# The shift of the routed rows added by TensorE, with shorter comparisons, in a hand-ordered two-layer trunk

## The reference, cut to what matters

```python
h = rms_norm(x, g) * (1 + scale) + shift          # scale and shift from the conditioning, one pair for context, one for latent
scores = sigmoid(h @ w_router)                    # 384 x 16
sel = (scores + b_router).reshape(-1, 4, 4)
best = argmax(sum(top_k(sel, 2)[0], -1), -1)      # the best of 4 groups by its two best scores
idx = best * 4 + top_k(sel[best], 2)[1]           # two experts of that group
w = scores[idx] / sum(scores[idx])
gate = sum(one_hot(idx, 16) * w[..., None], 1)
a = silu(h @ w_gate[e]) * (h @ w_up[e]) * gate[:, e]
y = sum over e of a @ w_down[e]
```

## Time and profile before

| | before |
|---|---|
| median of 3 runs | 1133.17 us (1132.31 to 1133.34) |
| the profiled execution | 1131.33 us |
| its span, first to last instruction | 1129.5 us |
| its mean granted TensorE clock | 0.978 |
| exponential of the route stage, layer 0 and layer 1 | 258.58 us and 793.74 us |
| first product of expert 0, layer 0 and layer 1 | 287.51 us and 818.45 us |

### The profile page before, as it was taken

How to read it: one execution, slowest core, us unless ns; L and a number is a source line. 1 busy time by engine, 2 the same in 40 slices (tenths; PEclk the granted TensorE clock), 3 DMA queues, 4 the chain that set the end, 5 groups by cost and what they waited for, 6 DMA issues and landing times.

```text
span 1129.5 us, 16096 instructions
## 1 busy us (share of the span) xinstructions
PE 1062.4 (94%) x5963; PEld 844.3 (75%) x5965; DVE 850.6 (75%) x1177; ACT 693.4 (61%) x885; POOL 181.8 (16%) x202
## 2 busy tenths in 40 slices
PE   7999998896999999999999999899699999999997
PEld 4798454683788888888868985568388888888876
DVE  5345656767999888888865546865899988888896
ACT  2323555652687777777724256755367777777764
POOL 0335200343111111110040011000301111111002
PEclk8999999997999999999999999999799999999998
DMA  9997888256999999999599463004799999999951
GB/s 353 345 345 220 321 300 282 71 171 258 354 370 365 368 376 375 373 374 386 212 389 280 149 188 128 1 1 152 299 362 375 367 370 384 375 375 369 367 195 58
DMA packets 83201, 321.99 MB, mean 285 GB/s; under 512 B 22560, under 2 KB 27054, under 8 KB 70332
## 3 DMA queue, kind: packets, MB, share of 16 engines
q1 hardware_dynamic: 67232, 285.58, 68.6%
q0 software_dynamic: 14800, 32.30, 8.5%
q10 hardware_dynamic: 1100, 3.23, 0.7%
HBM read 310.15 MB, written 30.59 MB: 302 GB/s over the span
## 4 chain that ended last, share of the span: by engine, by line
PE 84%; DVE 7%; ACT 4%; DMA 2%; issue 2%; SPq 1%; POOL 0%; DVEq 0%; ACTq 0%; POOLq 0%
PE bank L1266 16%; PE bank L1258 16%; PE bank L1259 16%; PE bank L1133 3%; PE bank L960 3%; PE bank L956 3%; PE bank L930 3%; PE bank L953 3%; PE bank L1319 2%; PE bank L1147 2%; DMA ring<-in_w_in 2%; PE bank L1025 2%; PE bank L1165 2%; PE bank L990 1%; PE bank L1066 1%
## 5 line engine op out<-in xcount | busy, mean ns | idle before, releaser
L1744 ACT ACTIVATE work_r<-ring 128x4096 fp32r<-128x4096 f32 x93 | 338.1, 3635 | 121.4 <-PE bank L1259 109.9
L2340 DVE TENSOR_TENSOR ring_r<-ring,work_r 128x4096 fp32r<-128x4096 f32 x92 | 404.2, 4417 | 2.8 <-ACT work_r L1744 2.8
L1258 PE MATMUL bank<-work_r 128*128 128x512 f32 x768 | 305.2, 397 | 4.7 <-issue 3.2
L1259 PE MATMUL bank<-work_r 128*128 128x512 f32 x768 | 300.1, 391 | 0.0
L1266 PE MATMUL bank<-ring_r,work_r 128*128 128x512 f32 x768 | 193.8, 394 | 0.0
L1258 PEld LDWEIGHTS bank<-work_r 128*128 128x128 f32 x768 | 144.8, 188 | 35.2 <-issue 4.0
L1266 PEld LDWEIGHTS bank<-ring_r,work_r 128*128 128x128 f32 x768 | 143.7, 188 | 32.4
L1259 PEld LDWEIGHTS bank<-work_r 128*128 128x128 f32 x768 | 144.4, 188 | 28.8
L2626 POOL DMA_INDIRECT work<-hscr,idx x32 | 39.9, 1247 | 280.9 <-PE bank L1319 253.5
L1587 ACT ACTIVATE work_r<-ring 128x512 fp32r<-128x512 f32 (+1 forms) x48 | 28.8, 603 | 71.4 <-PE bank L960 71.3
L2024 DVE TENSOR_TENSOR ring_r<-ring,work_r 128x512 fp32r<-128x512 f32 (+1 forms) x48 | 32.1, 676 | 50.7 <-ACT work_r L1587 50.6
(11 more groups left out here) (282 smaller groups left out, 1582.9 us busy)
## 6 DMA issues: line engine op xcount, KB each, us to landing
ring<-in_w_gate SPq DMA_DIRECT2D x32, 2048.0 KB, 10.1
ring<-in_w_up SPq DMA_DIRECT2D x32, 2048.0 KB, 10.2
ring<-in_w_down SPq DMA_DIRECT2D x32, 2048.0 KB, 10.4
ring<-in_w_ada SPq DMA_DIRECT2D x24, 2048.0 KB, 9.6
ring<-in_w_in SPq DMA_DIRECT2D x4, 2048.0 KB, 16.6
yscr<-hT POOLq DMA_DIRECT2D x2, 3072.0 KB, 12.8
ring<-yscr SPq DMA_DIRECT2D x6, 1024.0 KB, 7.2
ring<-in_w_out SPq DMA_DIRECT2D x4, 1280.0 KB, 6.5
```

The lines of the kernel that those rows point to most:

```text
L1258: mm(b[:], x_hi[:, k, :], hi[:, k, half, :], start=(k == 0), stop=False)
L1259: last = mm(b[:], x_lo[:, k, :], hi[:, k, half, :], start=False, stop=False)
L1744: A_(w_hi[:, slot % 2, :], ring[slot][:], ACT.Copy).then_inc(s_hi, 1)
L2340: tt(ring_r[slot][:], ring[slot][:], w_hi[:, slot % 2, :].bitcast(F32), ALU.subtract).then_inc(s_lo, 1)
```

## The change

The sums, the transposes and their order. TensorE now adds the shift: it turns the rows of one half of the columns for all three token tiles and leaves the banks open, then adds in each bank the product of one row: `inv_rows` (the reciprocal of `ns`, one value per token) times the row of the shift. ScalarE's copy multiplies by `ns`, so the shift itself comes out. `inv` is made by VectorE, turned by three small matmuls and copied by ScalarE. GpSimd's three additions and their semaphores are gone. ScalarE issues the store of each half row tile right behind its copy.

The shift's part of the logits: GpSimd folds `swr` by three halving additions, so that one matmul takes the place of eight.

The comparisons: who beats whom is taken as a difference of one masked comparison and its transpose, which saves one operation on 192 and one on 48 elements, and joins the two that followed.

The exponential stands before all row copies on ScalarE. The halves of expert 0's high part become quarters (two before `op6`, one before `op7`, one behind the stores); of the low part one quarter stands at `op6` and three in one operation behind `tokens_rest(0)`. The one-hots of part 3 go behind that operation, and `by_slot(3)` moves from the gate products to the `up` products. In layer 0 the fillers stand in another order. In layer 1, SP holds its third load (`w_up` of expert 1) until the first gather has landed, as layer 0 did before; until now layer 1 held only the load behind it.

```diff
-    return ["A010"], ["A011"], ["B010", "B011"], ["A18", "A19", "B18", "B19"]
+    return ["A010"], ["A011", "B010", "A18"], ["B011"], ["B18", "A19", "B19"]
...
-        n += ["router", "shiftw", "routerT"] + [f"hr{t}{h}" for t in range(NT) for h in range(2)]
+        n += ["router", "routerT"] + [f"hr{t}{h}" for h in range(2) for t in range(NT)]
...
-                            if p == 0 and isinstance(i, int) and (e, kind) == (1, 2 if l else 1):
+                            if p == 0 and isinstance(i, int) and (e, kind) == (1, 1):
                                 sp.wait_ge(gathers(l, 0)[0][0], gathers(l, 0)[1][0] + 16)
...
+                pe.wait_ge(s_swr, 6 * (l + 1))
+                mm(bW, ones, swr[:, 0, :], start=True, stop=True)
                 sums_of_added(l)
...
-                b = fill_begin((l, "shiftw"))
-                for k in range(KT):
-                    last = mm(b[:, 0:NT * NE], ones, swr[:, k, :], start=(k == 0), stop=(k == KT - 1))
...
-                    turn4((l, f"hr{t}{h}"), lambda k: hT[:, 4 * h + k, t * P:(t + 1) * P])
+                def rows_turned_half(h):
+                    pe.wait_ge(s_zgain, KT * l + 4 * h + 4)
+                    for t in range(NT):
+                        b = fill_begin((l, f"hr{t}{h}"))
+                        for k in range(4):
+                            mm(b[:, k * P:(k + 1) * P], hT[:, 4 * h + k, t * P:(t + 1) * P], ident, is_transpose=True,
+                               start=(k == 0), stop=False, skip_group_check=True)
+                def shift_added(h):
+                    for t in range(NT):
+                        r = slice(32 * t, 32 * t + 1)
+                        last = mm(bank((l, f"hr{t}{h}"))[:], inv_rows[r, :], shift_rows[1 if t == 0 else 0][r, 512 * h:512 * h + 512],
+                                  start=False, stop=True, skip_group_check=True)
+                        filled((l, f"hr{t}{h}"), last)
+                rows_turned_half(0)
+                pe.wait_ge(s_inv, 3 * l + 1)
+                for t in range(NT):
+                    last = mm(bI[32 * t:32 * t + 32, 0:P], inv[:, t:t + 1].to_broadcast([P, 32]), ident, start=True, stop=True,
+                              skip_group_check=True)
+                last.then_inc(s_inv, 1)
+                rows_turned_half(1)
+                pe.wait_ge(s_shin, 32 * (l + 1))
+                pe.wait_ge(s_inv, 3 * l + 3)
+                shift_added(0)
+                shift_added(1)
...
+                act.wait_ge(s_inv, 3 * l + 2)
+                A_(inv_rows[0:96, :], bI[0:96, 0:P], ACT.Copy).then_inc(s_inv, 1)
+                act.wait_ge(s_rexp, 2 * l + 1)
+                A_(rw[:, 0, :], rw[:, 0, :], ACT.Exp, scale=-1.0).then_inc(s_rexp, 1)
...
-                row_copies(0)
-                act.wait_ge(s_logit, l + 1)
-                A_(rw[:, 0, :], rw[:, 0, :], ACT.Exp, scale=-1.0).then_inc(s_rexp, 1)
-                row_copies(1)
-                row_copies(2)
-                row_store(0)
-                for j in route[0]:
-                    ada_row(l, j)
-                first_expert_high(l, 1).then_inc(s_hi, 1)
-                row_store(1)
-                row_store(2)
-                for j in route[1] + route[2] + route[3]:
+                for h in range(2):
+                    for t in range(NT):
+                        half = slice(512 * h, 512 * h + 512)
+                        copy((l, f"hr{t}{h}"), hrow[t][:, half], 512, scale=ns[:, 1, t:t + 1])
+                        read_out(act, (l, f"hr{t}{h}"))
+                        act.dma_start(hscr[t * P:(t + 1) * P, half], hrow[t][:, half]).then_inc(s_hscr, 16)
+                first_expert_high(l, 3)
+                act.wait_ge(s_feh, 4 * (l + 1))
+                act.sem_inc(s_hi, 1)
+                for j in (j for step in route for j in step):
                     ada_row(l, j)
...
-                    chain(tt(c1, spread4(x, "i"), spread4(x, "j"), ALU.is_equal))
+                    chain(tt(c1, spread4(x, "i"), spread4(x, "j"), ALU.is_ge))
                     chain(tt(c1, c1, before.unsqueeze(1).to_broadcast([P, n, EPG, EPG]), ALU.mult))
-                    chain(tt(c2, spread4(x, "i"), spread4(x, "j"), ALU.is_gt))
-                    chain(tt(c1, c1, c2, ALU.add))
-                    chain(nc.vector.tensor_reduce(g4(dst), c1, AX.X, ALU.add))
+                    chain(tt(c2, c1, c1.rearrange("p g j i -> p g i j"), ALU.subtract))
+                    chain(nc.vector.tensor_reduce(g4(dst), c2, AX.X, ALU.add))
+                    place_no = cv("iota")[:, 0:EPG].unsqueeze(1).to_broadcast([P, n, EPG])
+                    chain(stt(g4(dst), g4(dst), EPG - most, place_no, ALU.add, ALU.is_lt))
...
-                    for q in range(2, NPS if p else NPS - 1):
+                    for q in range(2, NPS if p else NPS - 2):
                         onehots(q)
...
-                    if p == 0:
-                        first_expert_low(0)
                     tokens_rest(0)
                     if p == 0:
-                        first_expert_low(1).then_inc(s_lo, 1)
+                        first_expert_low(1, 4).then_inc(s_lo, 1)
+                        onehots(NPS - 2)
                         onehots(NPS - 1)
...
+                for i, k in enumerate((KT // 2, KT // 4, KT // 8)):
+                    g.wait_ge(s_swr, 6 * l + NT + i)
+                    nc.gpsimd.tensor_tensor(swr[:, 0:k, :], swr[:, 0:k, :], swr[:, k:2 * k, :], ALU.add).then_inc(s_swr, 1)
...
-                for t in range(NT):
-                    read_out(g, (l, f"hr{t}0"))
-                    read_out(g, (l, f"hr{t}1"))
-                    nc.gpsimd.tensor_tensor(hrow[t], hrow[t], shift_rows[1 if t == 0 else 0], ALU.add).then_inc(s_hrow, 1)
```

More of the change, by code:

```diff
@@ L1302, in experts @@
                     by_slot(0)
+                    if p == 0:
+                        for j in route[3][0:1]:
+                            ada(j)
                     by_slot(1)
                     if p == 0:
-                        for j in route[3]:
+                        for j in route[3][1:]:
                             ada(j)
@@ L2160, in out_low, with first_expert_low @@
                     tt(w_low[:, x, c], w[:, x, c], out_hi[half].bitcast(F32), ALU.subtract).then_inc(s_outw_lo, 1)
-                def first_expert_low(half):
-                    v.wait_ge(s_hi, chunk_no(l, 0, 0, 0) + 1)
-                    x = slice(CW // 2 * half, CW // 2 * half + CW // 2)
+                def first_expert_low(first, end):
+                    v.wait_ge(s_feh, 4 * l + end)
+                    x = slice(CW // 4 * first, CW // 4 * end)
                     return tt(ring_r[0][:, x], ring[0][:, x], w_hi[:, 0, x].bitcast(F32), ALU.subtract)
@@ L2379, in experts @@
                     onehots(1)
+                    if p == 0:
+                        for j in route[1] + route[2]:
+                            ada(l, j)
                     slots(1)
                     if p == 0:
-                        for j in route[2]:
+                        for j in route[3][0:1]:
                             ada(l, j)
```

58 lines of the change are left out of this document (26 added, 32 removed).

## The result

| | before | changed |
|---|---|---|
| median | 1133.26 us (4 runs) | 1141.59 us (1140.37 to 1141.85, 4 runs) |
| profiled execution, its span | 1131.33, 1129.5 us | 1140.37, 1138.2 us |
| mean granted TensorE clock | 0.978 | 0.972 |

The ratio is 1.0075, 95% interval 1.0061 to 1.0089: slower, where 1129.7 was forecast, and outside the range. A second set of runs gave 1.0069 (1.0049 to 1.0088).

The account below looks back on a forecast made before the run. TensorE, busy 94%, was taken as the bound, with only its idle or slowed time in the two route stages winnable. Layer 0's 2.7 plus layer 1's 1.0 less 0.25 gave 3.45: median 1129.7 us, range 1125.8 to 1134.0.

Parts of the forecast that it names:

- T: Start of tokens_rest in each route stage; layer 0 forecast 280.3 to 281.4 instead of 286.77, layer 1 278.8 instead of 282.56.
- Before the mask: VectorE's route work: three long operations shrink by 5.65 without GpSimd's additions, and the mask ends at 262.5 instead of 269.8.
- Rival 4: VectorE's three long operations are long of themselves: mask at 268.2, costing 0.4 in layer 1, nothing in layer 0; no chance given.
- The shift on TensorE: Six one-row matmuls behind the transposes, 0.86 each, 5.2 us; they end at 263.9, A010 and A011 at 267.7.
- ScalarE: Six turns of copy, store issue and waits, 1.15 us each (1.0 to 1.5); A010's row copy ends at 268.2.
- From the rank to T, layer 0: B010, A18, rank at 271.0, gather 272.7, then A19, B19 and tokens: T at 280.3 to 281.4.
- Layer 1: Its route stage: T at 278.8 instead of 282.56, or 276.9 at full clock; half of the gather's 8 us store wait taken.
- What is given back: Behind T: VectorE's weights at T + 14.75, TensorE waits 3.2 us for them, 2.7 us lost per layer.
- GpSimd's halving: GpSimd's three small new additions may hold up VectorE in the op steps: 0.25 us for both layers.
- rival 3: Six stores on ScalarE's queue delay the fillers' row copies: slower from a turn of 1.45 us, up to 1137; chance 0.13.
- Rival 1: TensorE's clock stays full behind the rank: layer 0 gains 3.7, layer 1 2.9, median 1126.8; chance 0.22.
- Rival 2: Half stores end late, ScalarE's turn is 1.35, or the clock falls at A010: almost nothing won, 1132 to 1134; chance 0.20.

Follow-up runs that it names:

- c0: The changed kernel unaltered, run and profiled a second time: 1139.39 us, 1.0069 of the kernel before.
- x3: Changed kernel with ScalarE's copy of the first filler's row (A010, A110) moved from behind all six stores to behind the fourth: 1133.69 us, 1.0018.
- z5: Changed kernel with 18 unread matmuls filling TensorE's wait for the row copy, ahead of B010 and B110: 1142.03 us, 1.0078.
- y5: Changed kernel with 12 unread matmuls filling TensorE's wait for the weights of the slots: 1138.82 us, 1.006.
- x4: Changed kernel with GpSimd's three halving additions moved behind its masked bias of the next layer: 1139.12 us, 1.0066.
- y1: Changed kernel with both x1's move of the weights and x3's move of the row copy: 1123.44 us, 0.9927.
- x1: Changed kernel with VectorE's eight operations for the weights of the slots moved ahead of its wait for the rank: 1128.23 us, 0.9968.
- z2: y1 with three stores of whole rows (512 KB) in place of six of half rows: 1122.73 us, 0.9907.
- z4: z1 with SP in layer 0 also holding expert 1's gate weight until the first gather has landed: 1122.36 us, 0.9903.
- x2: Changed kernel with the one-hots of part 3 put back ahead of tokens_rest: 1131.19 us, 0.9993.
- y3: Changed kernel keeping shift, logits, comparisons, half-row stores and high-part quarters; filler order, part-3 one-hots, by_slot(3), SP's hold undone, low part partly: 1127.64 us, 0.9961.
- z1: y1 with layer 1's row copy of A111 also moved, to behind the fifth store: 1121.57 us, 0.9905.

## Why the prediction was wrong

Between the forecast (3.45 gained) and the first profile (8.73 lost) lie 12.2 us: 3.1 in T of layer 0, 0.8 in T of layer 1, 4.3 behind the weights, and the rest in two stretches that no term covered. For c0 the same parts are 4.8, 0.6, 3.2 and 2.1.

- **Before the mask: right.** L2264 and its neighbours fell to 0.2 to 0.5 us; the mask ends at 264.90 - 2.2 = 262.7, forecast 262.5. Rival 4 falls. The Trainium skill, "SBUF — State Buffer", SBUF: two separate sides, says that a VectorE operation with two SBUF inputs and a GpSimd operation that reads SBUF share one pair of ports, which the one that starts first holds for its whole instruction; this trace agrees (1.78 to 0.21 on 48 elements once GpSimd's additions are gone).
- **The shift on TensorE: mis-sized, on the good side.** I took 0.86 for each of six matmuls, 5.2; they take 2.0 together, since those of different row tiles run side by side. The Trainium skill, "TensorE: Matmul & The Clock Gate", Part 3: Packing small matmuls — row/col tiling, says that matmuls in different row groups overlap, which the prediction did not use. This trace agrees: three start within 0.01 us at 261.00.
- **ScalarE: right.** Turns 1.09 to 1.14 apart (forecast 1.15), A010's row copy ends at 270.70 - 2.2 = 268.5 (forecast 268.2).
- **From the rank to T, layer 0: the step that failed first.** I had TensorE busy until 267.7 and waiting half a microsecond; with the shift's real size it is done at 264.5 and idle for 4.04, until the row copy that comes when I had reckoned. So the overlap failed: work that I had laid over the row copy was not there. I had put half clock only behind the rank, and one job of it; in fact B010 and A18 ran at it already (4.6 together for 2.6), so the rank came 2.2 later than 271.0. From the rank to the gather I had 1.7 and it takes 3.0, and B011, which stands ahead of `by_slot(1)`, keeps TensorE waiting 2.39 for VectorE. T gained 2.3 to 0.6 instead of 5.4. x3 shows that the row copy's place is the cause; z5 shows that the clock at B010 and A18 alone is not, since the rank then comes at the forecast's time and T does not.
- **Layer 1: nearly right.** T gained 2.9 and 3.1 for 3.7. TensorE was done early here too, waited 4.18 for the row copy, and ran B110 and B111 at half clock (1.11 and 1.12). What the prediction calls layer 1's fillers of 4.05 (L1311) are ten matmuls that nobody reads. The gather did not wait for the stores: they land in 2.2 us there, 8.3 before. I had taken half of the 8.
- **What is given back: right in size, wrong in its end.** Weights 14.6 behind T (14.75 forecast), last product of `up` +2.7 in each layer. But the sum stopped at the wait's length. Behind it the clock fell, which cost another 1.6 to 2.7 in each layer, 4.3 in all in the profile after and 3.2 in c0; the trace of y5 takes just that away. It is a term that the sum lacked altogether.
- **GpSimd's halving: 0.25 forecast, nothing found** (x4).
- **What no term of mine covers:** layer 0's route starts 0.9 to 2.2 late, and the end of its experts costs 1.4 to 2.1. The first lies between -1.4 and +2.6 in the other kernels, with nearly the same work ahead of it. At the second, TensorE waits 2.4 to 3.4 us for nothing that the profile shows, before the change too (2.38). Behind it the clock falls in some executions and not in others; windows and waits say so (the changed kernel, then y1), but what decides it stays open. The expectations of x1 and c0 call it a wait of TensorE for its own code; no run shows that.

```profile
576.93 0.76 PE L1282 MATMUL bank<-work_r 128*128 128x512 f32 x1 [3.15 <-issue]
```

```profile
575.00:580.00 5.00, 3.07 (x7) 2.48 (x8) 3.10 (x2) 0.00 (x0) 0.21 (x1) 0.63 1.05 384
```

```profile
564.10 0.47 PE L1282 MATMUL bank<-work_r 128*128 128x512 f32 x1 [2.46 <-issue]
```

```profile
565.00:570.00 5.00, 5.00 (x25) 3.94 (x23) 2.85 (x3) 0.14 (x1) 0.57 (x1) 1.00 1.05 383
```

- **The rivals.** Slower came out, and the condition that rival 3 named was met in layer 0 (T gained 2.29 and 2.67 were given back), but not in layer 1 (2.91 and 2.70). Over both layers it makes 0.2 us and not 8.7, and its mechanism did not come, as the turn was not 1.45 or more. The stores on ScalarE's queue did delay the row copy, by what I had reckoned; what I had not reckoned is that TensorE would idle for it, and what an idle TensorE then does to its clock. Rival 1, full clock, was refuted by the windows. Rival 2's early fall of the clock, at A010, did come in some traces: A010 and A011 took 5.33 in z2 and 5.34 in z4 (there behind a wait of 1.65) and 3.64 in the other eleven of the changed kernels; in layer 1 the two jobs took 5.34 in c0, x2, x3, x4 and z2. In c0 it cost nothing there, since TensorE then waited 2.20 for the row copy instead of 4.18, and T gained 3.1. In c0, y3 and z2 the first twelve transposes of layer 0 took 2.7 to 2.8 us at half clock, and the second twelve 1.5 to 1.7: the clock came back in between. The Trainium skill, "TensorE: Matmul & The Clock Gate", Part 4: PE-mode transpose, says that the full clock does not engage for transposes, which do not count as busy in the same way. These rows do not agree: c0's granted clock was 0.50 from 257 to 259 and 1.00 from 260 to 261, with transposes and three small matmuls of 0.42 us on TensorE. Rival 2's six small stores did not land later than three large ones (7.5 us in y1, 8.7 in z2).

## What to carry to other kernels

When a change lets an engine wait less at one place, look at every list behind it that is worked off in order, and put each item where its user waits for it: here one row copy and eight small operations, moved, turned 0.75% slower into 0.7% faster (y1), 0.95% with one copy more (z1). Price a new wait of TensorE not by its length alone but also by the slow work behind it. And a term that was taken too large can hide a wait: check a sum again with its uncertain terms at their lower bound.

## What the runs showed of the hardware

- An idle stretch of 2.5 us of TensorE was followed by half clock, with 1.6 to 2.7 us of lost time; filled with matmuls that nobody reads, by none (y5). One of 0.74 us was followed by it as well (x2, layer 0, 1.5 us lost), one of 0.75 was not (x2, layer 1), and stretches of 2.4 to 2.5 us at the end of a loop were in some executions only.
- In c0 the granted clock came back from 0.50 to 1.00 while TensorE ran transposes, and in ten of thirteen profiles of changed kernels layer 0's 24 transposes ran at the full rate (1.47 and 1.53 us for twelve).
- Six matmuls of one row by 512 fp32 columns, in three row groups, took 2.0 us together; three at a time start within 0.01 us.
- Beside a load of 2 MB a store of 256 KB landed 7.1 to 8.1 us after its issue, without one 2.1 to 3.3 (medians of the six stores of a layer).
